# Which engine makes the low parts of PEER's query weights, and which bounds the forget gate

## The chip, the cores and the metric

One core of one Trainium2 chip runs the whole program in one launch. The metric is the device time of that core in microseconds (us); the number reported is the median of the runs. TensorE does matmuls, VectorE and GpSimd elementwise work (GpSimd can't reach PSUM here and is not asked to), ScalarE activations and copies with rounding, SyncE (SP) issues all loads.

## The reference, cut to what matters

Two blocks follow each other on 256 tokens of width 1024, in float32. The first has a mixer (gated linear attention and sparse attention), a cross attention and a PEER layer; the second has a mixer (HGRN2 and Hyena) and another PEER layer. Two places matter here.

A PEER layer computes queries from the normalized activations, scores them against sub-keys, picks 16 experts a head, and sums their outputs:

```
q = (xt @ wq).reshape(N, H, 2, PEER_DKEY // 2)
s = einsum('nhpd,hpkd->nhpk', q, subkeys)      # then top-k twice, softmax
act = gelu(einsum('cd,chkd->chk', xc, down[ec])) * gate
y   = einsum('chk,chkd->cd', act, up[ec])
```

The first PEER layer has 1024 query columns, the second 2048. The second mixer's forget gate is, for forward and backward and for each of 8 heads of 128 channels:

```
logf = log(lb + (1.0 - lb) * sigmoid(z))
k    = (1.0 - lb) * sigmoid(-z)
```

## The kernel before

Activations lie with channels on the partitions: 8 chunks of 128 channels by 256 tokens. Every weight matrix is cut into units of 512 KB (128 partitions by 1024 values). Float32 precision is kept by splitting: a value is the sum of a high part (rounded to fp32r) and a low part (the rest), and a product is three matmuls, L370 (high x high), L371 and L372. A unit of 128 output channels takes 8 chunks x 3 = 24 matmuls of 256 columns.

A unit goes through four hands (`Split`, from L315): SP loads it into one of 3 ring slots (L334), ScalarE copies it rounded to the high part (L338), then an engine subtracts: ring minus high gives the low part. That is VectorE at L343 or GpSimd at L349, as `c.low_by` says when the unit is planned. The ring slot is free when the low part is made. High and low go to one of 3 pairs of buffers, free when TensorE is done with the unit. Two units are fetched ahead of the one that is multiplied (`AHEAD = 2`). A `Whole` unit (L312) is not split; its matmuls (L402) take it from the ring slot in plain float32.

A program is a list of steps in one order. Each engine walks through that list and does its share of each step, with semaphore waits between engines; so the list fixes the order on each engine, and an engine that waits holds up everything behind it.

`late_channels` (L436) runs a projection whose input norm is not known yet: matmuls of the unnormalized activations start at once, and the evacuation `Late` (L552, VectorE) multiplies what is in PSUM by the reciprocal root. The first two units of such a stage are fetched ahead by the stage before it. After the second, `Rstd` (L623, L630, L625) computes the norm. From unit 2 on, evacuations alternate with the steps that `make_norm` gave, spread over the units: here the eight chunks of `NormalizeChunk`, each L711 on VectorE (h times gain times norm), L718 on ScalarE (high part) and L714 on VectorE (low part). L711 and L714 read two operands from SBUF; L552 reads one from PSUM and one from SBUF.

`late_channels` is used in three stages that matter:

- PEER 1 queries (`peer`, 8 units): two chunks a unit, units 2 to 5.
- The keys of the second mixer (16 units): the evacuation is `HgrnKeys`, that is L552, ScalarE's two sigmoids L2327 and L2328, and GpSimd's three instructions L2332 (one_minus times z plus lb), L2333 (one_minus times k) and L2335 (z at least 2^-62). `HgrnLogs` (L2346) takes the logarithm later, of all heads at once. Beside the chunks there are eight `NormInPlace` (L698, VectorE, two SBUF operands), in turns with them.
- PEER 2 queries (`peer`, 16 units): one chunk a unit, units 2 to 9.

Behind the queries `peer` flushes the first two units of the expert table `down`, so they too are split by whatever `c.low_by` says then. Before, that is VectorE; the change to GpSimd comes after the routing is planned, for the rest of the 128 units of `down`. During `down` the routing (top-k) runs on VectorE.

Of the kernel before, what the change touches and what calls it, by code (L numbers as in the profile page):

```python
# [32 lines left out]
ALU = mybir.AluOpType  # L33
ACT = mybir.ActivationFunctionType
# [90 lines left out]
class Step:  # L125
# [10 lines left out]
    def scalar(self, q):  # L136
        pass
# [4 lines left out]
    def pool(self, q):  # L142
        pass
# [292 lines left out]
def late_channels(c, srcs, acts, evac, make_norm, beside=()):  # L436


    beside, waiting = list(beside), []

    def make(unit, n):
        step = c.plan(LateChannels(c, unit, acts, evac(n)))
        waiting.append(step)
        if n == 1:
            beside.extend(make_norm())
        if n >= 1:
            while waiting:
                c.plan(waiting.pop(0))
        if n >= 2:
            for _ in range(-(-len(beside) // max(1, len(srcs) - 2 - n))):  # L450
                c.plan(beside.pop(0))

    for n, src in enumerate(srcs):
        c.submit(src, lambda unit, n=n: make(unit, n))
# [69 lines left out]
class Keep(Evac):  # L524
# [5 lines left out]
    def out_of_psum(self, c):  # L530
        self.kept = c.mark("kept")
        c.last_kept = self.kept
        return self.kept
# [1645 lines left out]
def peer(c, h, xn, work, tmp, gained, squares, name, gain, half_dim, wq, subkeys, down, up, following=()):  # L2179

    n_q = 2 * PEER_H * half_dim // P
    with ExitStack() as ctx:
        x = Experts()
        x.experts = c.sb(name + "_experts", [P, NKEYS, T], ctx)
        x.gates_high = c.sb(name + "_gates_high", [P, T], ctx, F32R)
        free = work[:, :, :].rearrange("p k t -> p (k t)")
        x.pairs, x.gates_low = free[:, 0:2 * T].rearrange("p (a t) -> p a t", a=2), free[:, 2 * T:3 * T]
        x.copy = free[:, 3 * T:3 * T + GROUP * NKEYS].rearrange("p (n t) -> p n t", t=GROUP)
        first_kept = 70
        area = x.experts[:, first_kept:NKEYS, :].rearrange("p a t -> p (a t)")  # L2190
        sk = area[:, 0:n_q * P].rearrange("p (k n) -> p k n", k=n_q)
        qs = area[:, n_q * P:n_q * (P + T)].rearrange("p (k t) -> p k t", k=n_q)
        sk_came = c.load(sk, subkeys, after=[c.last_product])

        def norm():
            c.plan(SumSquares(c, squares, KD - 1))
            c.plan(Rstd(c, tmp[:, :]))
            return [NormalizeChunk(c, h, gain, work, tmp[:, :], xn, k) for k in range(KD)]

        late_channels(c, [wq[n] for n in range(n_q)], gained, lambda n: Late(qs[:, n, :], 1.0, c), norm)  # L2200
        c.flush(down[0], down[1])
        r = Routing(c, area[:, n_q * (P + T):], half_dim, qs, sk, [c.last_kept, sk_came], x.pairs, x.gates_high, x.gates_low)
        x.iota_copied = r.iota_copied = c.plan(CopyIota(c)).copied
        routes = [Route(c, r, i) for i in range(NT)]
        for i in range(4):
            c.bank_free[i] = (routes[1].kept,)
        c.bank_free[6] = (routes[1].kept,)
        places = {3: routes[0:1], 5: routes[1:2], 39: routes, 41: routes}
        x.there, x.gated, x.stored, x.routed = 0, 0, None, r.kept
        c.rotation = [4, 5]  # L2210
        c.low_by = "pool"
        with ExitStack() as inner:
            x.first = c.sb(name + "_first_keys", [P, 2, GROUP, P], inner, F32R)
            x.second = c.sb(name + "_second_keys", [P, 2, GROUP, 2, P], inner, F32R)
            x.hot_free, x.low_made, x.copy_free = [(), ()], None, None
            n_groups, used, finished, first = T // GROUP, 0, 0, 43
            onehots = []
            for n in range(NKEYS):
                for route in places.get(n, ()):
                    c.plan(route)  # L2220
                due = n_groups * (n - first + 1) // (NKEYS - 2 - first)
                new = len(onehots)
                while len(onehots) < min(due, n_groups):
                    onehots.append(c.plan(Onehots(c, x, len(onehots))))
                c.channels(down[n], xn, Hidden(x, n, (r.kept,) if n >= first_kept else ()))
                while used < new:
                    spread = c.plan(Spread(c, x, used, onehots[used]))
                    c.plan(ApplyGates(c, x, used, spread))
                    used += 1
                while finished < len(onehots):  # L2230
                    c.plan(onehots[finished])
                    finished += 1
            c.low_by = "vector"
            c.flush(up[0], up[1])

        x.n_coef = 2
        x.coef = c.sb(name + "_coef", [P, x.n_coef, 2, T], ctx, F32R)
        x.coef_free = [tuple(x.hot_free[0] + x.hot_free[1])] * x.n_coef
        coefs = [None] * NKEYS
        for n in range(NKEYS):  # L2240
            def make(unit, n=n):
                if n == NKEYS - 2:
                    coefs[n + 1] = c.plan(Coef(c, x, n + 1))
                c.plan(UpUnit(c, x, unit, n, coefs[n]))

            if n == 0:
                coefs[0] = c.plan(Coef(c, x, 0))
            elif n >= c.AHEAD:
                coefs[n - c.AHEAD + 1] = c.plan(Coef(c, x, n - c.AHEAD + 1))
            c.submit(up[n], make)  # L2250
        c.flush(*following)
# [56 lines left out]
class HgrnKeys(Evac):  # L2308
# [6 lines left out]
    def out_of_psum(self, c):  # L2315
        self.late = Late(self.z, 1.0, c)
        taken = self.late.out_of_psum(c)
        self.sigmoids, self.scaled = c.mark("hg_sigmoids"), c.mark("hg_scaled")
        self.bounded = c.last_bounded = c.mark("hg_bounded")
        return taken  # L2320

# [3 lines left out]
    def scalar(self, q, out, done):  # L2325
        q.wait_ge(self.late.scaled)
        q.e.activation(self.k, self.z, ACT.Sigmoid, scale=-1.0)  # L2327
        q.e.activation(self.z, self.z, ACT.Sigmoid).then_inc(*self.sigmoids.once())  # L2328

    def pool(self, q, out, done):  # L2330
        q.wait_ge(self.sigmoids, self.bound_ready)
        q.e.tensor_scalar(self.z, self.z, self.one_minus, self.lb, ALU.mult, ALU.add).then_inc(*self.scaled.once())  # L2332
        q.e.tensor_scalar(self.k, self.k, self.one_minus, None, ALU.mult)  # L2333
        q.wait_ge(self.scaled)
        q.e.tensor_scalar(self.z, self.z, 2.0 ** -62, None, ALU.max).then_inc(*self.bounded.once())  # L2335


# [727 lines left out]
def program(nc, dram, out):  # L3065
    with ExitStack() as ctx:
# [27 lines left out]
        with ExitStack() as shared:  # L3094
# [3 lines left out]
            squares = cross_attention(c, h, xn, work, tmp, mem_kv, spare, squares,  # L3098
                                      [dram["peer_wq"][0], dram["peer_wq"][1]])
        peer(c, h, xn, work, tmp, spare, squares, "peer_1", c.gain("norm_ffn"), 64, dram["peer_wq"], dram["peer_subkeys"],  # L3100
             dram["peer_down"], dram["peer_up"], [dram["w_in_2"][8], dram["w_in_2"][9]])

# [13 lines left out]
        def two_norms():  # L3116
            for k in range(KD):
                c.plan(SumGained(c, by_gain, squared[k], k))
            for k in range(KD):
# [6 lines left out]
        c.rotation = list(range(6))  # L3126
        spare, squares = second_mixer(c, h, xn, work, gained, two_norms, [dram["peer_w_q_2"][0], dram["peer_w_q_2"][1]])
        peer(c, h, xn, work, tmp, spare, squares, "peer_2", c.gain("norm_ffn_g_2"), 128, dram["peer_w_q_2"],
             dram["peer_subkeys_2"], dram["peer_u_2"], dram["peer_v_2"])
        with ExitStack() as between:  # L3130
# [115 lines left out]
```

## Time and profile before

| what | value |
|---|---|
| median of 3 runs | 2531.92 us (2531.15 to 2541.61) |
| the profiled execution | 2539.18 us, span 2537.4 us |
| TensorE, VectorE, ScalarE, GpSimd busy | 94%, 65%, 53%, 31% of the span |
| low parts on VectorE (L343) | 398, mean 1228 ns |
| low parts on GpSimd (L349) | 276, mean 2442 ns |
| a 512 KB load, issue to landing | 3.6 us (median, PEER 2 query weights) |
| mean granted TensorE clock | 0.966 |

Busy time is what instructions of an engine cover; a busy TensorE isn't one at its peak. Times in rows are from the start of the span. In a timeline row the first number is the start, the second the duration from the first instruction's start to the last one's end (x2 means two instructions merged), and brackets hold the idle time of the engine before it and what ended it.

### The profile page before, as it was taken

The page shows a single profiled execution, that of the slowest core. Times are in us where ns is not written, and L with a number is a line of the kernel's source. Part 1 is how long each engine was busy: PE and PEld are TensorE (multiplying, and loading weights), DVE is VectorE, ACT ScalarE, POOL GpSimd, SP SyncE. Part 2 cuts the span into 40 slices and gives each one's busy share as a digit, 9 for nine tenths or more (in the row PEclk, how much of TensorE's full clock was granted, in tenths as well). Part 3 has the DMA queues.
Part 4 walks back from the last instruction along what each step waited for, and adds up shares of the span by engine and source line. Part 5 has one row for each costly group of instructions (what it writes and reads, how often), then busy time and mean ns, then how long its engine had stood idle before and what let it go on. Part 6 is the DMA issues. An engine that isn't in the chain of part 4 may idle for free.

```text
span 2537.4 us, 39066 instructions
## 1 busy us (share of the span) xinstructions
PE 2375.6 (94%) x15354; PEld 2140.5 (84%) x15354; DVE 1660.1 (65%) x3193; ACT 1343.1 (53%) x2494; POOL 775.4 (31%) x404
## 2 busy tenths in 40 slices
PE   6878898999999999998888988899999999999998
PEld 5876788999999888886857976799999999788886
DVE  4564456977777556665667384666977778555555
ACT  3345344468887454444433444244468888444443
POOL 3000002877776000000800152101877777000000
PEclk8888899999999999999999998999999999999999
DMA  5322234555555656664332342254555555565563
GB/s 172 124 95 69 92 100 149 176 176 165 165 164 170 185 191 192 192 192 128 125 116 93 116 148 95 67 165 151 183 175 166 162 164 169 180 189 186 189 187 120
DMA packets 108287, 383.36 MB, mean 151 GB/s; under 512 B 12976, under 2 KB 15841, under 8 KB 107529
## 3 DMA queue, kind: packets, MB, share of 16 engines
q1 hardware_dynamic: 108104, 380.86, 47.3%
q8 instruction: 123, 2.02, 0.3%
q14 instruction: 60, 0.48, 0.1%
HBM read 379.74 MB, written 1.06 MB: 150 GB/s over the span
## 4 chain that ended last, share of the span: by engine, by line
PE 81%; DVE 11%; ACT 4%; DMA 2%; issue 2%; POOL 0%; SPq 0%; DVEq 0%; ACTq 0%; POOLq 0%
PE psum L370 23%; PE psum L372 22%; PE psum L371 22%; PE psum L2021 2%; PE psum L402 2%; DVE weight_parts L343 2%; ACT weight_parts L338 2%; PE psum L607 1%; PE psum L2466 1%; PE psum L2686 1%; PE psum L1457 1%; PE psum L1018 1%; PE psum L1357 0%; DVE hg_tmp L1064 0%; PE psum L2611 0%
## 5 line engine op out<-in xcount | busy, mean ns | idle before, releaser
L349 POOL TENSOR_TENSOR weight_parts<-weight_ring,weight_parts 128x1024 fp32r<-128x1024 f32 x276 | 670.8, 2442 | 506.5 <-ACT weight_parts L338 506.0
L370 PE MATMUL psum<-acts_high,weight_parts 128*128 128x256 f32 x2744 | 794.1, 289 | 23.4 <-DVE weight_parts L343 11.2
L338 ACT ACTIVATE weight_parts<-weight_ring 128x1024 fp32r<-128x1024 f32 x674 | 710.6, 1055 | 150.1 <-PE psum L372 79.2
L372 PE MATMUL psum<-acts_high,weight_parts 128*128 128x256 f32 x2744 | 782.6, 285 | 0.0
L371 PE MATMUL psum<-acts_low,weight_parts 128*128 128x256 f32 x2744 | 782.1, 285 | 0.0
L343 DVE TENSOR_TENSOR weight_parts<-weight_ring,weight_parts 128x1024 fp32r<-128x1024 f32 x398 | 488.4, 1228 | 296.1 <-ACT weight_parts L338 295.5
L370 PEld LDWEIGHTS psum<-acts_high,weight_parts 128*128 128x128 f32 x2744 | 532.1, 194 | 34.6 <-issue 12.5
L371 PEld LDWEIGHTS psum<-acts_low,weight_parts 128*128 128x128 f32 x2744 | 532.4, 194 | 1.4 <-issue 0.5
L372 PEld LDWEIGHTS psum<-acts_high,weight_parts 128*128 128x128 f32 x2744 | 532.4, 194 | 0.0
L370 PE MATMUL psum<-weight_parts,peer_coef 128*128 128x512 f32 x1024 | 405.9, 396 | 4.0 <-issue 3.9
L372 PE MATMUL psum<-weight_parts,peer_coef 128*128 128x512 f32 x1024 | 404.8, 395 | 0.0
L371 PE MATMUL psum<-weight_parts,peer_coef 128*128 128x512 f32 x1024 | 402.8, 393 | 0.0
L2103 ACT ACTIVATE peer_coef<-peer_experts 128x256 fp32r<-128x256 f32 x256 | 106.8, 418 | 356.5 <-PE psum L372 355.4
L370 PEld LDWEIGHTS psum<-weight_parts,peer_coef 128*128 128x128 f32 x1024 | 193.4, 189 | 46.5 <-issue 4.2
L372 PEld LDWEIGHTS psum<-weight_parts,peer_coef 128*128 128x128 f32 x1024 | 193.3, 189 | 45.3
L371 PEld LDWEIGHTS psum<-weight_parts,peer_coef 128*128 128x128 f32 x1024 | 193.2, 189 | 44.3
L2107 DVE TENSOR_TENSOR peer_coef<-peer_experts,peer_coef 128x256 fp32r<-128x256 f32 x256 | 108.5, 425 | 153.6 <-ACT peer_coef L2103 153.6
L2002 ACT ACTIVATE peer_second_keys<-psum,work 128x128 fp32r<-128x128 f32 x512 | 146.2, 371 | 14.9 <-DVE peer_second_keys L1993 13.7
L585 POOL TENSOR_TENSOR work<-h 128x256 f32<-128x256 f32 x32 | 19.4, 614 | 410.7 <-DVE h L569 399.5
L2082 ACT ACTIVATE peer_experts<-psum 128x256 f32<-128x256 f32 (+35 forms) x250 | 78.2, 313 | 121.1 <-PE psum L372 121.0
L1990 DVE TENSOR_TENSOR psum<-psum,work 128x512 f32<-128x512 f32 x128 | 89.2, 697 | 59.7 <-ACT peer_second_keys L2002 58.6
L370 PE MATMUL psum<-acts_spare_high,weight_parts 128*128 128x256 f32 x352 | 103.2, 293 | 16.9 <-DVE weight_parts L343 16.8
(426 smaller groups left out, 3135.4 us busy)
## 6 DMA issues: line engine op xcount, KB each, us to landing
weight_ring<-in_peer_down SPq DMA_DIRECT2D x128, 512.0 KB, 3.6
weight_ring<-in_peer_up SPq DMA_DIRECT2D x128, 512.0 KB, 3.5
weight_ring<-in_peer_u SPq DMA_DIRECT2D x128, 512.0 KB, 3.6
weight_ring<-in_peer_v SPq DMA_DIRECT2D x128, 512.0 KB, 3.5
weight_ring<-in_w_in SPq DMA_DIRECT2D x88, 512.0 KB, 3.6
weight_ring<-in_w_out SPq DMA_DIRECT2D x16, 512.0 KB, 3.6
weight_ring<-in_peer_w_q SPq DMA_DIRECT2D x16, 512.0 KB, 3.6
weight_ring<-in_w_in_v SPq DMA_DIRECT2D x10, 512.0 KB, 3.6
```

The lines of the kernel that those rows point to most:

```text
L338: q.e.activation(self.high, self.ring, ACT.Copy).then_inc(*self.rounded.once())
L343: q.e.tensor_tensor(self.low, self.ring, self.high.bitcast(F32), ALU.subtract).then_inc(*self.unit.ready.once())
L349: q.e.tensor_tensor(self.low, self.ring, self.high.bitcast(F32), ALU.subtract).then_inc(*self.unit.ready.once())
L370: q.e.matmul(out, sh, mh, start=first, stop=False)
L371: q.e.matmul(out, sh, ml, start=False, stop=False)
L372: return q.e.matmul(out, sl, mh, start=False, stop=last)
L402: last = q.e.matmul(self.out, w[:, k, :], acts.whole[:, k, :], start=k == 0, stop=k == KD - 1)
L1990: q.e.tensor_tensor(ones, iota, over(x.pairs[:, 1, tokens], P, 2), ALU.is_equal).then_inc(*self.marked.once())
L2002: last = q.e.activation(self.second[:, t, 1, :], self.c.bank(6)[:, P * t:P * t + P], ACT.Copy, bias=0.0, scale=x.gates_low[:, token:token ...
L2082: last = q.e.activation(self.x.experts[:, self.n, n:T], out[:, n:T], ACT.Gelu_apprx_tanh)
L2103: q.e.activation(self.high, self.src, ACT.Copy).then_inc(*self.rounded.once())
L2107: q.e.tensor_tensor(self.low, self.src, self.high.bitcast(F32), ALU.subtract).then_inc(*self.ready.once())
```

## The change

The line `c.low_by = "pool"` in `peer` moves up, ahead of the query projection, so that query units 2 and up and the first two units of `down` are split by GpSimd. In `HgrnKeys` the instruction z = one_minus * z + lb moves from GpSimd (L2332) to ScalarE, as an Identity activation with scale and bias from memory, behind a wait for ScalarE's own sigmoid. GpSimd's multiplication of k stays and no longer has the other ahead of it; its maximum waits for the Identity.

```diff
@@ peer
+        c.low_by = "pool"
         late_channels(c, [wq[n] for n in range(n_q)], gained, lambda n: Late(qs[:, n, :], 1.0, c), norm)
         c.flush(down[0], down[1])
...
         c.rotation = [4, 5]
-        c.low_by = "pool"
@@ HgrnKeys
-        self.sigmoids, self.scaled = c.mark("hg_sigmoids"), c.mark("hg_scaled")
+        self.sigmoids, self.forgets = c.mark("hg_sigmoids"), c.mark("hg_forgets")
...
         q.e.activation(self.z, self.z, ACT.Sigmoid).then_inc(*self.sigmoids.once())
+        q.wait_ge(self.sigmoids, self.bound_ready)
+        q.e.activation(self.z, self.z, ACT.Identity, bias=self.lb, scale=self.one_minus).then_inc(*self.forgets.once())
 
     def pool(self, q, out, done):
         q.wait_ge(self.sigmoids, self.bound_ready)
-        q.e.tensor_scalar(self.z, self.z, self.one_minus, self.lb, ALU.mult, ALU.add).then_inc(*self.scaled.once())
         q.e.tensor_scalar(self.k, self.k, self.one_minus, None, ALU.mult)
-        q.wait_ge(self.scaled)
+        q.wait_ge(self.forgets)
         q.e.tensor_scalar(self.z, self.z, 2.0 ** -62, None, ALU.max).then_inc(*self.bounded.once())
```

## Rows read from the trace of the kernel before

**Rows 1.** Busy by window: length, then PE, PEld, DVE, ACT, POOL; clock, DMA.

```profile
398.97:417.73 18.76, 12.00 (x96) 11.21 (x97) 12.79 (x25) 8.45 (x14) 0.00 (x0) 1.00 0.33 113
...
1717.08:1740.79 23.71, 21.40 (x169) 19.99 (x169) 16.65 (x29) 10.53 (x15) 0.00 (x0) 1.00 0.49 156
1740.79:1751.80 11.01, 11.01 (x97) 11.01 (x98) 7.67 (x10) 4.25 (x4) 0.00 (x0) 1.00 0.77 226
...
1223.56:1254.60 31.04, 27.23 (x217) 25.62 (x218) 19.41 (x33) 16.38 (x33) 29.57 (x28) 1.00 0.48 153
1254.60:1282.20 27.60, 27.60 (x130) 24.31 (x129) 18.12 (x25) 8.30 (x12) 7.97 (x9) 1.00 0.44 134
```

**Rows 2.** Timeline of VectorE, one unit of PEER 2's queries.

```profile
1719.19 1.23 DVE L343 TENSOR_TENSOR weight_parts<-weight_ring,weight_parts 128x1024 fp32r<-128x1024 f32 x1 [0.53 <-ACT weight_parts L338]
1720.33 0.42 DVE L552 SCALAR_TENSOR_TENSOR peer_experts<-psum,tmp 128x256 f32<-128x256 f32 x1
1720.67 0.47 DVE L711 SCALAR_TENSOR_TENSOR work<-h,gains,tmp 128x256 f32<-128x256 f32 x1
1721.62 0.43 DVE L714 TENSOR_TENSOR acts_low<-work,acts_high 128x256 fp32r<-128x256 f32 x1 [0.48 <-ACT acts_high L718]
1722.58 1.23 DVE L343 TENSOR_TENSOR weight_parts<-weight_ring,weight_parts 128x1024 fp32r<-128x1024 f32 x1 [0.52 <-ACT weight_parts L338]
```

**Rows 3.** Timeline of ScalarE in the same unit.

```profile
1721.17 0.42 ACT L718 ACTIVATE acts_high<-work 128x256 fp32r<-128x256 f32 x1 [2.02 <-DVE work L711]
1721.50 1.04 ACT L338 ACTIVATE weight_parts<-weight_ring 128x1024 fp32r<-128x1024 f32 x1
```

**Rows 4.** Waits of TensorE, 1207.5 to 1254.6: us in total, times, longest.

```profile
PE psum L370 <- DVE weight_parts L343: 4.2, 9, 0.7
```

**Rows 5.** Timeline of VectorE, keys: the first and last of eleven low parts.

```profile
1214.77 1.37 DVE L343 TENSOR_TENSOR weight_parts<-weight_ring,weight_parts 128x1024 fp32r<-128x1024 f32 x1
...
1250.47 1.23 DVE L343 TENSOR_TENSOR weight_parts<-weight_ring,weight_parts 128x1024 fp32r<-128x1024 f32 x1 [0.53 <-ACT weight_parts L338]
```

**Rows 6.** Timeline of GpSimd: low parts beside VectorE's work.

```profile
418.39 3.01 POOL L349 TENSOR_TENSOR weight_parts<-weight_ring,weight_parts 128x1024 fp32r<-128x1024 f32 x1 [32.74 <-ACT weight_parts L338]
...
1499.35 4.72 POOL L349 TENSOR_TENSOR weight_parts<-weight_ring,weight_parts 128x1024 fp32r<-128x1024 f32 x2 [5.46 <-ACT weight_parts L338]
```

**Rows 7.** Timeline of ScalarE, then TensorE: unit 2 of PEER 2's queries.

```profile
1705.56 1.06 ACT L338 ACTIVATE weight_parts<-weight_ring 128x1024 fp32r<-128x1024 f32 x1 [5.19 <-DMA weight_ring<-in_peer_w_q]
...
1707.92 0.39 PE L370 MATMUL psum<-acts_spare_high,weight_parts 128*128 128x256 f32 x1 [2.04 <-DVE weight_parts L343]
```

**Rows 8.** Timeline of VectorE beside the low parts of Rows 6.

```profile
417.93 1.22 DVE L343 TENSOR_TENSOR weight_parts<-weight_ring,weight_parts 128x1024 fp32r<-128x1024 f32 x1
...
1500.28 0.48 DVE L2806 SCALAR_TENSOR_TENSOR hy_u<-psum,gains,hy_u 128x255 f32<-128x255 f32 x1
...
1502.46 1.89 DVE L1065 SCALAR_TENSOR_TENSOR work<-work,gains,hg_tmp 128x256 f32<-128x256 f32 x1
```

**Rows 9.** Timeline of ScalarE, keys: the second sigmoid and what follows.

```profile
1231.49 0.40 ACT L2328 ACTIVATE hg_zf<-hg_zf 128x256 f32<-128x256 f32 x1
1231.80 1.04 ACT L338 ACTIVATE weight_parts<-weight_ring 128x1024 fp32r<-128x1024 f32 x1
```

**Rows 10.** Timeline of VectorE: L678 waits for VectorE's own L677.

```profile
1201.94 0.41 DVE L677 TENSOR_SCALAR both<-psum 128x256 f32<-128x256 f32 x1
1202.39 0.42 DVE L678 SCALAR_TENSOR_TENSOR both<-tmp,both 128x256 f32<-128x256 f32 x1
```

**Rows 11.** Timeline of ScalarE: an Identity with scale and bias from memory, its follower.

```profile
1477.68 0.55 ACT L2796 ACTIVATE hy_x<-psum,gains 128x256 f32<-128x256 f32 x1
1478.13 0.71 ACT L1040 ACTIVATE hg_sq<-work 128x256 f32<-128x256 f32 x2
```

**Rows 12.** Timeline of GpSimd, then VectorE, in the keys.

```profile
1213.34 0.85 POOL L2335 TENSOR_SCALAR hg_zf<-hg_zf 128x256 f32<-128x256 f32 x1
...
1213.82 0.43 DVE L714 TENSOR_TENSOR acts_low<-work,acts_high 128x256 fp32r<-128x256 f32 x1 [0.71 <-ACT acts_high L718]
```

## Prediction

> **What bounds the kernel now.** I read the page's busy shares first (TensorE 94% of the span), which says little about three stretches of some 30 us, so I went to the stretches that the diff touches, with busy time by window [rows 1]. "Unit" is one weight block of 512 KB: a load, a high part on ScalarE (L338), a low part (L343 on VectorE, L349 on GpSimd), 24 matmuls. Where nothing holds TensorE up, four units take 11.01 us, 2.75 each, TensorE busy throughout at a granted clock of 1.00 (as in all five windows). PEER-1's query stage (398.97 to 417.73, 4 units) needs 4.69 a unit and TensorE works 12.00 of 18.76; PEER-2's (1717.08 to 1740.79, 7 units) 3.39 a unit. Both wait for a low part on VectorE. The period is a ring of VectorE and ScalarE, each of which takes its instructions in order, to be seen in the timeline [rows 2, 3]: L343 starts 1719.19, L552 1720.33, L711 1720.67, ScalarE's L718 1721.17, its next L338 1721.50, the next L343 1722.58: 3.39. PEER-1 has two norm chunks (L711, L718, L714) a unit, hence 4.69.
>
> The third stretch is the forget-gate keys. TensorE waits for L343 nine times, once a unit [rows 4]. Its ring is L343, L552, ScalarE's two sigmoids L2327 and L2328, perhaps L718, then L338 and L343 again: ten periods in 1250.47 - 1214.77 = 35.70 us [rows 5]. GpSimd is nearly full here (29.57 of 31.04) but nobody on the ring waits for it. Behind it TensorE is busy for all 27.60 us [rows 1], so what the keys lose is lost to the end.
>
> **Part 1, low parts on GpSimd.** Prefetched units 0 and 1 of each query stage stay on VectorE; 6 + 14 query units and 2 + 2 units of the first expert table move: 24 L343 at 1.23 us go, 24 L349 at about 2.4 come (4.72 for two [rows 6]). No load is added. SP's queue gets its slot free about 1.2 us later per unit; three slots against a load of 3.6 (median of the page's list of loads), L338 of 1.05 and 2.4 make 7.1 / 3 = 2.4 us a unit, under 2.75, so the queue is covered.
>
> If GpSimd and VectorE ran side by side the ring would lose 1.2 us. Unit 2 would start 1.2 later (L338 begins 1705.56, TensorE 1707.92 [rows 7]; +1.17 for 2.4 instead of 1.23), then run at 2.75 to 2.8: PEER-2's first expert unit at 1709.1 + 14 x 2.8 = 1748.3 against 1751.8, 3.5 gained. In PEER-1 the ring of evacuation and two chunks takes 2.92 (L552 0.34, twice L711 to L714 0.95 and L714 0.34); following units 5, 6, 7 and the first expert unit through gives 412.2 against 417.73, 5.5 gained.
>
> But the rows say they don't run side by side. GpSimd's two L349 from 1499.35 end at 1504.07; VectorE's L1065, two operands in SBUF, issued at 1502.46, takes 1.89, where the like L711 takes 0.47 [rows 2], and ends 0.28 after that, while L2806 at 1500.28, whose other operand is in PSUM, takes its 0.48 [rows 6, 8]. The other way round, L349 at 418.39 behind L343 (417.93, 1.22) takes 3.01 and ends 2.25 after it. So L711 and L714 (both operands in SBUF) wait for a running L349, L552 (PSUM) doesn't. The Trainium skill, SBUF — State Buffer, "Who interferes with whom", says the same: a VectorE instruction with two SBUF inputs contends with a GpSimd instruction that reads SBUF, and the later one blocks fully; by this rule the 9.0 us above are not to be had.
>
> Worked through from these durations. PEER-2: let L711 be issued at L. By [rows 2, 3] L711 comes L718 + 0.45 (L714) + 0.34 + 0.34 = 1.13 after L718, GpSimd's low part 0.33 + 1.08 = 1.41 after it, so L711 is first by 0.28 and the low part runs L+0.48 to L+2.73. L714, issued L+0.96, ends L+3.01. Having waited, it goes ahead of the next low part, which runs to L+5.26. The next L711, issued L+3.27, ends L+5.54; L718 L+5.57; L714 L+6.02, free; L552 L+6.36; L711 L+6.70. Two units in 6.7: 3.35 each, against 3.39. From the first chunk (L = 1715.45 once unit 4's low part has held chunk 0 back) unit 12 starts 1740.85 + 0.2 for handshakes, against 1740.79, then 11.0 us to the experts: +0.3. PEER-1: with two chunks a unit the same steps give L711 at L+2.95 for the second chunk, L718 L+3.46, L714 L+3.91, L552 L+4.25, the next L711 L+4.59: 4.59 against 4.69; unit 5 starts 0.2 late, the first expert unit 0.3 early. Part 1 together: 0. Bounds: -9.0 with no blocking; +9.4 if L711 loses the race each time. Then a period is 0.3 + 0.37 + 1.08 + 2.4 = 4.15 in PEER-2 (8 x 0.77 = 6.1) and 5.5 in PEER-1 (4 x 0.82 = 3.3). I take 0, the race being won by 0.28. No L711 or L714 of before runs beside an L349, so the order of issue is worked out, not seen.
>
> **Part 2, the bound on ScalarE.** L2332 leaves GpSimd 16 times, which nobody misses. ScalarE gets one Identity a unit, which first waits for its own sigmoid. Before, what follows L2328 starts 0.31 after it [rows 9]. Now: the sigmoid's full 0.40, 0.04 for an engine's wait on itself (L677 takes 0.41 and L678 starts 0.45 after it [rows 10]), then the Identity. With scale and bias from memory it has a pitch of 0.45 (L2796 at 1477.68, next at 1478.13 [rows 11]). 0.40 + 0.04 + 0.45 - 0.31 = 0.58 a unit. Queued behind it are L718 and L338, for which VectorE and TensorE wait. L338 of units 5 to 15 follows the Identities of 2 to 12: 11 x 0.58 = 6.4. Those of units 0 and 1 are hidden, since VectorE then waits for TensorE to end unit 2, whatever ScalarE does. L343 lasts 1.37 at 1214.77 and 1.23 at 1250.47 [rows 5]; less GpSimd work beside it may return 0.05 a unit in some eight of them, 0.4. Bounds: 11 x 0.31 = 3.4 if the wait is free, 11 x 0.64 = 7.0 if it costs 0.1. I take +6.0. The later logarithms and scans lie beside the 27.60 us of matmuls.
>
> A block would be possible here too. Counted from L552, the new ring has the sigmoid's end at 1.18, L2333 on GpSimd from 1.2 to 2.15, the Identity's end at 1.77, L2335 from 2.25 to 3.10, L714 at 2.12, L698 issued at 2.46 and L343 due at 3.06. If L2335 held VectorE over its whole recorded span, L698 would end at 3.4 and L343 start 0.3 late in the eight units with a chunk, +2.4. But L714 at 1213.82 takes its usual 0.43 although L2335 is recorded from 1213.34 to 1214.19 [rows 12]: a 256-element GpSimd instruction doesn't hold VectorE over its recorded span. I take 0 for it. The same section of the Trainium skill has the lock last for the whole instruction, which this row doesn't bear out.
>
> **Sum.** 0 + 6.0 = +6.0 on the profiled execution: span 2537.4 to 2543.4, its time 2539.2 to 2545.2. It was 7.3 above the median of the runs, by more than the change; I carry the difference to the median: 2531.9 + 6.0 = 2538. About 0.5% (12.7 us) is what can be told from no change.
>
> **Rivals.**
> No blocking in the query stages (the low parts then run beside the chunks): -9.0 + 6.0 = -3, 2529. For it: L714 beside L2335. Against: L1065's 1.89. Chance 0.15.
> L711 loses the race: L711 starts only when a low part ends, and every period is a serial chain of both engines. +9.4 + 6.0 = +15.4, 2547, slower. It decides when L711 is issued after L349, that is from 0.28 us of delay on VectorE. For it: the margin is small and rests on pitches. Against: after a block L714 and L552 bring L711 into step again. Chance 0.10.
> The Identity is hidden, because GpSimd's relief shortens the ring: 0, 2532. For it: GpSimd is 95% busy. Against: the ring holds no GpSimd instruction. Chance 0.12.
> L2335 holds L698 in the keys for its whole span: 6.0 + 2.4 = +8.4, 2540. Against it: L714 beside L2335. The Trainium skill's section named above would have it so. Chance 0.08.
>
> **How the numbers follow.** Forecast 0.55: 2538, within 0.5%. Range: down to the first rival, 2528, up to the second, 2548; the shown runs lie 10 us apart, which is in it too. Faster by over 0.5%: only with luck of the runs, 0.03. Slower by over 0.5%: the second rival, and a little of the forecast with high runs, 0.11. Same 0.86.
>
> **What would show it.** The first low part of the first expert table is in L349. L711 and L714 have maxima near 2.4 us in the query stages, alternating with normal ones, and the period of PEER-2 stays at 3.3 to 3.4, with TensorE waiting for L349. In the keys the period of L343 grows by 0.58, the last key unit starts some 6 us later counted from 1207.57, and GpSimd no longer lags. Wrong would be: periods of 2.8 in the queries; 4 or more there; or the keys' ten periods still at 35.7.

## The result, and the profile after

The changed kernel takes 2541.01 us (median of 20 runs, 2536.46 to 2548.06) against 2533.27 us for the kernel before on the same chip (20 runs, 2529.99 to 2541.61). The ratio is 1.0028 with a 95% interval of 1.0020 to 1.0035, so the change costs 7.1 us (5.1 to 8.9). The predicted 2538 was +6.0 on the base of that time, 2531.9. One of run 12's twelve executions took 3015.4 us at a granted clock of 0.72, against about 0.96 in all others, and is left out of its ratio.

The two profiled spans differ by less, 2538.7 against 2537.4 us, and that must be cleared up before any row is compared. From PEER-2's first expert unit to the end of the span, where TensorE is as busy in both and the change touches only one low part that nobody waits for, before took 785.6 us and after 777.2. Of the fourteen executions profiled in this study (a kernel run twice counts twice), two took 785.6 and twelve 777.2 to 778.9, for kernels that are the same there. The profiled execution of before was one with a slow last stretch, which fits its 7.3 us above the median. So I read the change stage by stage. A query stage is counted from TensorE's first matmul with `acts_spare` to its first with `acts_high`, which is the first expert unit; the keys from the stage's first L343 to TensorE's first L402.

| stage, us | before | after | difference | predicted |
|---|---|---|---|---|
| PEER-1's queries | 33.15 | 32.62 | -0.5 | -0.3 |
| PEER-2's queries | 52.35 | 54.17 | +1.8 | +0.3 |
| the keys | 64.97 | 71.11 | +6.1 | +6.0 |
| sum | | | +7.4 | +6.0 |

The sum lies within the interval of the measured 7.1.

**PEER-2's queries.** First the timeline of the three engines (start, length, engine, line, tiles; in brackets the idle time before and who ended it), from the evacuations of units 2 and 3 to a full pair of units. Line numbers below 2200 are those of before.

```profile
1721.45 0.42 DVE L552 SCALAR_TENSOR_TENSOR peer_experts<-psum,tmp 128x256 f32<-128x256 f32 x1 [1.55 <-PE psum L372]
1721.79 0.47 DVE L711 SCALAR_TENSOR_TENSOR work<-h,gains,tmp 128x256 f32<-128x256 f32 x1
...
1723.75 2.40 POOL L349 TENSOR_TENSOR weight_parts<-weight_ring,weight_parts 128x1024 fp32r<-128x1024 f32 x1 [2.33 <-ACT weight_parts L338]
1724.18 0.42 DVE L552 SCALAR_TENSOR_TENSOR peer_experts<-psum,tmp 128x256 f32<-128x256 f32 x1 [1.00 <-PE psum L372]
1724.52 1.91 DVE L711 SCALAR_TENSOR_TENSOR work<-h,gains,tmp 128x256 f32<-128x256 f32 x1
...
1727.59 0.47 DVE L711 SCALAR_TENSOR_TENSOR work<-h,gains,tmp 128x256 f32<-128x256 f32 x1
1727.91 4.93 POOL L349 TENSOR_TENSOR weight_parts<-weight_ring,weight_parts 128x1024 fp32r<-128x1024 f32 x2 [1.76 <-ACT weight_parts L338]
...
1728.55 2.04 DVE L714 TENSOR_TENSOR acts_low<-work,acts_high 128x256 fp32r<-128x256 f32 x1 [0.48 <-ACT acts_high L718]
1730.36 0.38 PE L370 MATMUL psum<-acts_spare_high,weight_parts 128*128 128x256 f32 x1 [0.78 <-POOL weight_parts L349]
1730.51 0.41 DVE L552 SCALAR_TENSOR_TENSOR peer_experts<-psum,tmp 128x256 f32<-128x256 f32 x1
1730.85 2.28 DVE L711 SCALAR_TENSOR_TENSOR work<-h,gains,tmp 128x256 f32<-128x256 f32 x1
...
1733.61 0.43 DVE L714 TENSOR_TENSOR acts_low<-work,acts_high 128x256 fp32r<-128x256 f32 x1 [0.48 <-ACT acts_high L718]
```

Against [rows 2] the low part has left VectorE, and what it left behind is waiting. From 1727.59 on, L711 takes 0.47, 2.28, 0.47 and so on, and L714 takes 2.04 after a short L711 and 0.43 after a long one. A long one ends 0.28 us or so after the low part that it met (1723.75 + 2.40 = 1726.15; 1724.52 + 1.91 = 1726.43). This is the alternation that was worked out ahead, with 6.7 us for a pair of units: every second unit of TensorE starts at 1730.36, 1737.07, 1743.76 and 1750.44, which makes pairs of 6.71, 6.69 and 6.68.

What is new stands before it. Three windows of TensorE (columns as in [rows 1]) around unit 2's start:

```profile
1712.00:1717.00 5.00, 1.91 (x14) 1.51 (x14) 0.42 (x1) 3.48 (x4) 2.60 (x2) 1.00 0.64 260
1717.00:1721.00 4.00, 4.00 (x23) 4.00 (x23) 2.51 (x3) 1.28 (x2) 4.00 (x2) 0.58 0.60 169
1721.00:1725.00 4.00, 4.00 (x37) 4.00 (x36) 2.06 (x5) 1.37 (x2) 1.67 (x2) 0.99 0.60 228
```

and the wait ahead of them:

```profile
1716.80 0.39 PE L370 MATMUL psum<-acts_spare_high,weight_parts 128*128 128x256 f32 x1 [3.09 <-POOL weight_parts L349]
```

TensorE waits 3.09 us for unit 2's low part, where it waited 2.04 before [rows 7]. Then the granted clock falls to the lower of its two levels, 1.2 GHz, for most of 4 us (0.50 over 1717.64 to 1721.05): 23 matmuls in 4 us instead of 37, and 14 x 4 / 37 = 1.5 us lost. Before, the same unit ran at the upper level:

```profile
1708.00:1712.00 4.00, 4.00 (x35) 4.00 (x36) 3.48 (x4) 2.59 (x3) 0.00 (x0) 1.00 0.64 197
```

The late matmuls also made L552 wait for TensorE, for unit 2 until 1721.45 and for unit 3 until 1724.18. So the second L711 was issued after the low part of 1723.75, lost the race for the order of issue once, and took 1.91.

**PEER-1's queries** run at 4.53 us a unit (TensorE starts units at 403.09, 407.62, 412.15 and 416.68), every second L714 at 2.02 to 2.04, and no L711 is held. TensorE's waits from 398 to 417 us:

```profile
PE psum L370 <- POOL weight_parts L349: 5.1, 4, 1.5
```

The granted clock fell once in this stage too, behind unit 2, although TensorE had waited only 1.89 us for it (a window from its start on):

```profile
392.38:396.38 4.00, 4.00 (x22) 4.00 (x23) 2.47 (x3) 2.40 (x3) 3.80 (x2) 0.61 0.57 156
```

In the second profile of the same kernel (run 10) the wait was 2.00 us and the clock stayed at 1.00. That stage is 0.4 us shorter there.

**The keys.** The timeline of one unit without a chunk, ScalarE, GpSimd and VectorE:

```profile
1242.09 0.42 ACT L2327 ACTIVATE hg_kb<-hg_zb 128x256 f32<-128x256 f32 x1 [1.63 <-DVE hg_zb L552]
1242.41 0.40 ACT L2328 ACTIVATE hg_zb<-hg_zb 128x256 f32<-128x256 f32 x1
1242.85 0.60 ACT L2330 ACTIVATE hg_zb<-hg_zb,hg_lb,hg_one_minus 128x256 f32<-128x256 f32 x1
1242.90 0.94 POOL L2334 TENSOR_SCALAR hg_kb<-hg_kb,hg_one_minus 128x256 f32<-128x256 f32 x1 [2.23 <-ACT hg_zb L2328]
1243.35 1.05 ACT L338 ACTIVATE weight_parts<-weight_ring 128x1024 fp32r<-128x1024 f32 x1
1243.91 0.85 POOL L2336 TENSOR_SCALAR hg_zb<-hg_zb 128x256 f32<-128x256 f32 x1
1244.43 1.23 DVE L343 TENSOR_TENSOR weight_parts<-weight_ring,weight_parts 128x1024 fp32r<-128x1024 f32 x1 [1.99 <-ACT weight_parts L338]
```

The Identity (L2330) starts 0.44 after its sigmoid, and L338 follows it 0.50 later; in [rows 9] L338 followed the sigmoid by 0.31. The units with a chunk now come every 4.25 us and those without every 3.94 (before 3.68 and 3.30), so ten periods take 1256.86 - 1215.33 = 41.53 us against the 35.70 of [rows 5]. GpSimd, which was nearly full, waits for ScalarE over 2 us a unit and nobody gains by it. TensorE's waits in the stage (us in total, times, longest), where [rows 4] had 4.2 in 9:

```profile
PE psum L370 <- DVE weight_parts L343: 10.4, 10, 1.2
```

### The profile page after: what moved, and what is told of

It reads as the page before. It is cut to its first block, busy times and chain, and to the rows that moved or that the text cites. A ratio compares the mean times of both kernels' runs of the same rounds, so it can differ in the third digit from the quotient of the medians.

```text
span 2538.7 us, 39067 instructions
## 1 busy us (share of the span) xinstructions
PE 2370.9 (93%) x15354; PEld 2141.9 (84%) x15354; DVE 1648.0 (65%) x3169; ACT 1352.5 (53%) x2510; POOL 812.3 (32%) x412
## 3 DMA queue, kind: packets, MB, share of 16 engines
q8 instruction: 123, 2.02, 0.3%
## 4 chain that ended last, share of the span: by engine, by line
PE 81%; DVE 11%; ACT 4%; issue 2%; DMA 2%; POOL 1%; SPq 0%; DVEq 0%; ACTq 0%; POOLq 0%
PE psum L370 23%; PE psum L372 22%; PE psum L371 22%; PE psum L2021 2%; PE psum L402 2%; DVE weight_parts L343 1%; PE psum L607 1%; ACT weight_parts L338 1%; PE psum L2687 1%; PE psum L2467 1%; POOL weight_parts L349 1%; PE psum L1457 1%; PE psum L1018 1%; DVE acts_low L714 1%; PE psum L1357 0%
## 5 line engine op out<-in xcount | busy, mean ns | idle before, releaser
L349 POOL TENSOR_TENSOR weight_parts<-weight_ring,weight_parts 128x1024 fp32r<-128x1024 f32 x300 | 727.2, 2436 | 456.1 <-ACT weight_parts L338 455.8
L338 ACT ACTIVATE weight_parts<-weight_ring 128x1024 fp32r<-128x1024 f32 x674 | 710.5, 1055 | 147.1 <-PE psum L372 73.9
L343 DVE TENSOR_TENSOR weight_parts<-weight_ring,weight_parts 128x1024 fp32r<-128x1024 f32 x374 | 458.4, 1227 | 277.4 <-ACT weight_parts L338 277.3
```

The costliest lines, as they stand in the source:

```text
L338: q.e.activation(self.high, self.ring, ACT.Copy).then_inc(*self.rounded.once())
L343: q.e.tensor_tensor(self.low, self.ring, self.high.bitcast(F32), ALU.subtract).then_inc(*self.unit.ready.once())
L349: q.e.tensor_tensor(self.low, self.ring, self.high.bitcast(F32), ALU.subtract).then_inc(*self.unit.ready.once())
```

## The experiments

All were timed in five rounds beside the kernel before. "Stages" are the three differences to before in the order of the table above. The unedited rest moved between executions: the start by up to 9 us, and the stretch from the keys to PEER-2 by some 4. So a time tells some 3 to 4 us apart, a stage some 0.7.

**1. Part 1 alone.** Only the move of `c.low_by = "pool"`.

```diff
+        c.low_by = "pool"
         late_channels(c, [wq[n] for n in range(n_q)], gained, ...
...
-        c.low_by = "pool"
```

> Part 1 alone: the low parts of both query stages on GpSimd, the keys as before. Theory (GpSimd's low part and VectorE's L711/L714 exclude each other, the order settles into a fixed alternation; the traces of before and after differ by -0.53 us in PEER-1's queries and +1.83 in PEER-2's): +1.3 us against before, pairs of units 6.7 us apart in PEER-2. Rival, no blocking: -9. Rival, L711 loses every time: +9.4.

Measured: ratio 1.0001 (0.9987 to 1.0016), +0.3 us (-3.3 to +4.1); stages -1.0, +1.8, -0.3. PEER-2's L711 takes up to 2.28 and L714 up to 2.06. Both rivals lie outside the interval: the stages together neither gain 9 us nor lose them.

**2. Part 2 alone.** Only the edits in the keys.

> Part 2 alone: the Identity on ScalarE, the query stages' low parts on VectorE. Theory (11 periods of the keys' ring grow by the sigmoid's full length, the engine's wait on itself and the Identity's pitch, 0.57 to 0.64 each): +6.2 us. Rival, the stretch is hidden by TensorE: 0. Rival, the wait on itself is free: 11 x 0.31 = +3.4.

Measured: 1.0031 (1.0016 to 1.0046), +7.9 us (+4.1 to +11.7); stages -0.1, -0.1, +6.5, ten periods 41.53 us. Hidden, and a free wait, are outside the interval. Nearly the whole loss is this part's.

**3 and 4. The lock taken away.** In run 3 the chunks' product and a copy of the rms factor lie in PSUM and the low parts stay on VectorE; in run 4 the low parts move as well.

```diff
+class ChunkInPsum(NormalizeChunk):
...
+        self.x, self.gain, self.out, self.tmp = x[:, k, :], gain[:, k:k + 1], c.bank(7)[:, 0:T], c.bank(7)[:, T:2 * T]
...
+class RstdCopied(Rstd):
...
+        q.e.reciprocal(self.tmp, self.tmp).then_inc(*self.ready.once())
+        q.wait_ge(self.ready)
+        settle(self.c, q, "vector", q.e.tensor_copy(self.c.bank(7)[:, T:2 * T], self.tmp))
...
-            return [NormalizeChunk(c, h, gain, work, tmp[:, :], xn, k) for k in range(KD)]
+            return [ChunkInPsum(c, h, gain, xn, k) for k in range(KD)]
```

> The kernel before with the norm chunks' product and its rms factor in a PSUM bank, so that L711 and L714 each have one operand in SBUF; low parts stay on VectorE. This is the control of the next run. Theory: no GpSimd instruction contends in the query stages before, so nothing changes but the lengths: one copy of about 0.4 us twice, and up to 0.1 us a chunk if the PSUM operand is slower: 0 to +1.5 us.

Measured: 1.0013 (0.9998 to 1.0029); stages -0.3, +0.3, +0.1. This was the other execution with 785.6 us in the last stretch. By its stages the move into PSUM by itself is worth nothing.

> Part 1 alone, with the product and the rms factor of the norm chunks in PSUM. If the exclusion of L349 against two-SBUF-operand instructions is what took the gain: L711 and L714 stay near 0.5 us at their longest, PEER-2's units come every 2.75 to 2.8 us (first expert unit 3.5 us earlier), PEER-1's every 2.9 to 3.2 (5.5 us earlier), together about -9 + 1 = -8 us. Rival, VectorE is held whatever its operands' place: +1.3 to +3, pairs of 6.7 us stay. Rival, the period was bound by something else (ScalarE's order, the slots): periods above 3.2 in PEER-2 with short L711 and L714.

Measured: 0.9974 (0.9958 to 0.9989), -6.6 us (-10.7 to -2.8); stages -5.0, -2.9, +0.2. The timeline of PEER-2's queries:

```profile
1716.23 2.41 POOL L349 TENSOR_TENSOR weight_parts<-weight_ring,weight_parts 128x1024 fp32r<-128x1024 f32 x1 [0.32 <-ACT weight_parts L338]
1716.68 0.42 DVE L552 SCALAR_TENSOR_TENSOR peer_experts<-psum,tmp 128x256 f32<-128x256 f32 x1 [1.02 <-PE psum L372]
1717.02 0.48 DVE L711 SCALAR_TENSOR_TENSOR psum<-h,gains,psum 128x256 f32<-128x256 f32 x1
...
1717.95 0.42 DVE L714 TENSOR_TENSOR acts_low<-psum,acts_high 128x256 fp32r<-128x256 f32 x1 [0.45 <-ACT acts_high L718]
1718.95 2.40 POOL L349 TENSOR_TENSOR weight_parts<-weight_ring,weight_parts 128x1024 fp32r<-128x1024 f32 x1 [0.31 <-ACT weight_parts L338]
```

L711 is issued 0.79 us into a running low part and takes 0.48; both are as short as alone. The period is 2.72, L552 waits for TensorE in every unit, and TensorE is the bound. Against the pair above each has one operand fewer in SBUF. L711's output left SBUF as well, but in run 9 below it is back there and L711 still takes 0.47, so it is the inputs that count. With that the exclusion is shown, and where part 1's gain went. The Trainium skill, SBUF — State Buffer, "Who interferes with whom", says that a VectorE instruction with at most one SBUF input, outside the modes that use two ports, does not contend with GpSimd; these rows agree. PEER-1 gained 5.0 of the expected 5.5 us and PEER-2 2.9 of 3.5. TensorE's wait for unit 2 was 3.25 us here and the clock fell as in the changed kernel (0.73 over 1702 to 1708).

**5 and 6. The price on ScalarE.** In run 5 ScalarE takes k's multiplication, whose sigmoid came first; in run 6 both steps.

```diff
-        q.wait_ge(self.sigmoids, self.bound_ready)
-        q.e.activation(self.z, self.z, ACT.Identity, bias=self.lb, scale=self.one_minus).then_inc(...)
+        q.wait_ge(self.first, self.bound_ready)
+        q.e.activation(self.k, self.k, ACT.Copy, bias=0.0, scale=self.one_minus).then_inc(...)
```

> The changed kernel, but the multiplication that ScalarE takes over is that of k by one_minus, whose sigmoid came first, and z's two-pointer step stays on GpSimd. If 0.13 of the 0.64 us a unit is ScalarE waiting for the sigmoid just before, that part goes: ten periods of L343 take 41.53 - 1.3 = 40.2 us, +4.7 in the keys against before, about +6 in all. Rival, the wait is no part of the price: 41.5 us stay. Rival, a shorter list of pointer operands makes the instruction cheaper too: under 39.5.

> The changed kernel with both steps on ScalarE: k by one_minus, then z's Identity, which by then need not wait; GpSimd keeps the maximum alone. Theory (the keys' ring grows by the pitches on ScalarE, whatever GpSimd is relieved of): 0.51 + 0.51 a unit, ten periods 35.70 + 9.6 = 45.3 us, some +10.3 in the keys and +11.5 in all, so about 1.0045. Rival, GpSimd's relief gives something back on the ring (L343 shorter, no contention): under 44.

Measured: run 5 0.9997 (0.9982 to 1.0011), stages -0.9, +2.4, +3.6, ten periods 1252.06 - 1212.89 = 39.17 us; run 6 1.0023 (1.0009 to 1.0037), stages -0.7, +2.0, +9.0, ten periods 44.08. Timeline of ScalarE in run 6, one unit:

```profile
1238.52 0.40 ACT L2329 ACTIVATE hg_zb<-hg_zb 128x256 f32<-128x256 f32 x1
1238.83 0.49 ACT L2331 ACTIVATE hg_kb<-hg_kb,hg_one_minus 128x256 f32<-128x256 f32 x1
1239.23 0.59 ACT L2333 ACTIVATE hg_zb<-hg_zb,hg_lb,hg_one_minus 128x256 f32<-128x256 f32 x1
1239.72 0.40 ACT L718 ACTIVATE acts_high<-work 128x256 fp32r<-128x256 f32 x1
```

Both misses have one cause: the step with one pointer operand has a pitch of 0.40 (1238.83 to 1239.23), not the 0.51 that I had given it, and the Identity with two pointers 0.49. Neither waits for the sigmoid, since 0.31 after the last sigmoid's start there was other work to do. So the Identity's 0.64 is 0.13 of waiting and 0.51 of pitch; run 5's 0.40 a unit is what the rival with the shorter list of pointers had said (the step is also a Copy and no Identity, which these runs don't separate). In run 6 the ring grows by 0.40 + 0.49 = 0.89 (3.30 to 4.19) and GpSimd's further relief gives nothing back beyond the first 0.07.

**7. The race, made to be lost.** Part 1 alone, with two short VectorE instructions ahead of each L711.

```diff
+        q.e.tensor_scalar(self.spare[:, 0:T], self.tmp, 1.0, None, ALU.mult)
+        q.e.tensor_scalar(self.spare[:, T:2 * T], self.tmp, 1.0, None, ALU.mult)
         super().vector(q)
```

> Part 1 alone, with two short VectorE instructions (rms factor into an unused PSUM bank, one SBUF operand each) ahead of every L711, which issue it at least 0.4 us later. If the race decides: L711 loses each time, PEER-2's units with a chunk come every 4.15 us instead of 3.35 and PEER-1's every 5.5 instead of 4.53, together 7 to 9 us slower than part 1 alone, +8 to +11 against before. Rival, the alternation is stable against such a delay: periods grow by the added instructions at most, to 3.75 in PEER-2, +3 in all.

Measured: 1.0038 (1.0020 to 1.0056), +9.6 us (+5.1 to +14.2); stages +5.6, +7.5, -0.1. Two units of PEER-2, GpSimd and VectorE:

```profile
1736.70 2.37 POOL L349 TENSOR_TENSOR weight_parts<-weight_ring,weight_parts 128x1024 fp32r<-128x1024 f32 x1 [1.76 <-ACT weight_parts L338]
1737.04 2.31 DVE L711 SCALAR_TENSOR_TENSOR work<-h,gains,tmp 128x256 f32<-128x256 f32 x1
...
1740.82 2.37 POOL L349 TENSOR_TENSOR weight_parts<-weight_ring,weight_parts 128x1024 fp32r<-128x1024 f32 x1 [1.76 <-ACT weight_parts L338]
1741.16 2.32 DVE L711 SCALAR_TENSOR_TENSOR work<-h,gains,tmp 128x256 f32<-128x256 f32 x1
```

L711 is issued 0.34 us after the low part and loses in every unit; the period is 4.12 to 4.13. The serial chain of the second rival is real. The two instructions add nothing to it but the later issue: L711 ends 0.28 us after the low part. In PEER-1 units come every 6.18 us, above the expected 5.5, because the second chunk's two instructions stand in the ring too. With that the stages come to +13.0, above the expected 8 to 11.

**8 and 11. Unit 2's low part left on VectorE**, on top of run 4 (`low_from` is 3).

```diff
     for n, src in enumerate(srcs):
+        if n == low_from:
+            c.low_by = "pool"
         c.submit(src, lambda unit, n=n: make(unit, n))
```

> Part 1 with the chunks' product and rms factor in PSUM, and unit 2 of each query stage left on VectorE, which is idle then. Expected from 2.4 against 1.23 us for the first low part that TensorE waits for: the stage of PEER-1 26.9 us instead of 28.1, PEER-2's 48.3 instead of 49.5, so 2.4 us more than the run without this, about -9 to -10 against before (0.9963). Rival, the units behind it then wait for GpSimd and give it back: no better than -6.6.

> The kernel with the chunks' product and rms factor in PSUM and unit 2 on VectorE once more. By its stages -3.8 (of which 1.9 were lost to a lower granted clock in one unit) and -3.9: -8 to -10 us against before, not the -14.5 first measured.

Measured: 0.9943 (0.9925 to 0.9961) and 0.9963 (0.9950 to 0.9976), -14.5 and -9.4 us; stages -3.8, -3.9, -0.3 and -3.7, -4.6, -0.3. PEER-2 gains another 1.0 us over run 4 in run 8 and 1.7 in run 11, and its clock holds, as the wait and two windows of run 8 show:

```profile
1704.11 0.38 PE L370 MATMUL psum<-acts_spare_high,weight_parts 128*128 128x256 f32 x1 [2.06 <-DVE weight_parts L343]
```

```profile
1702.00:1706.00 4.00, 1.95 (x17) 1.89 (x17) 1.72 (x3) 3.75 (x5) 1.84 (x1) 1.00 0.53 183
1706.00:1710.00 4.00, 4.00 (x37) 4.00 (x37) 3.51 (x6) 1.16 (x3) 2.97 (x2) 1.00 0.75 240
```

PEER-1 lost 1.2 us to run 4 instead of gaining 1.2, and 1.3 in run 11. In both, TensorE had to wait 2.49 us for unit 5, against 2.23 in run 4, so part of what unit 2 had gained was given back, as the rival says. The clock then fell, which it had not done in run 4:

```profile
400.00:403.00 3.00, 1.85 (x12) 1.85 (x13) 2.06 (x6) 1.72 (x3) 2.35 (x2) 0.83 0.25 42
403.00:406.00 3.00, 3.00 (x18) 3.00 (x18) 0.93 (x3) 1.33 (x2) 2.38 (x2) 0.60 0.64 172
```

This is the fastest version of the study: some 10 us under the kernel before, and 0.5% under the changed one (0.9963 against 1.0014, timed side by side).

**9. Only the rms factor in PSUM**, the rest as in run 8: L711 has one SBUF operand, L714 again two.

> As the run with unit 2 on VectorE, but only the rms factor lies in PSUM: L711 has one SBUF operand, L714 again two. If it is L711's place ahead of ScalarE's high parts that matters, and L714 may wait as long as L552 has to wait for TensorE anyway: in PEER-2 L714 takes up to 1.1 us and the units still come every 2.7 to 2.8 us, the stage 48.5 to 49.5; in PEER-1 the second chunk's L711 stands behind a held L714, so the period is 4.0 to 4.5 and the stage 31 to 32. Together -4 to -5 us against before. Rival, any held instruction brings the 3.35 back: PEER-2 at 52 or more, about -1 in all.

Measured: 0.9966 (0.9953 to 0.9979), -8.6 us (-11.9 to -5.3); stages -0.3, -4.1, 0.0. Timeline of PEER-2 (L713 and L716 are L711 and L714 two lines further down):

```profile
1732.64 0.47 DVE L713 SCALAR_TENSOR_TENSOR work<-h,gains,psum 128x256 f32<-128x256 f32 x1
...
1733.60 0.97 DVE L716 TENSOR_TENSOR acts_low<-work,acts_high 128x256 fp32r<-128x256 f32 x1 [0.48 <-ACT acts_high L720]
1734.60 2.41 POOL L349 TENSOR_TENSOR weight_parts<-weight_ring,weight_parts 128x1024 fp32r<-128x1024 f32 x1 [0.30 <-ACT weight_parts L338]
1735.02 0.42 DVE L554 SCALAR_TENSOR_TENSOR peer_experts<-psum,tmp 128x256 f32<-128x256 f32 x1 [0.45 <-PE psum L372]
```

The low half of the chunk is held for half a microsecond and costs nothing, because the evacuation behind it has to wait for TensorE anyway. The period is 2.72 as in run 4. In PEER-1, where the second chunk stands behind the held instruction, the period stays at 4.52 and the stage takes 32.9 us; 4.0 to 4.5 and 31 to 32 were expected. So in PEER-2 it is enough to free L711, the one that ScalarE's high parts hang on. The time is 4 us below what the stages say (-4.4), and its interval excludes them.

**10 and 12. Two kernels again**, the changed one and that of run 5.

> The changed kernel once more, on the same chip as the other three, since the times of the runs before came out up to 5 us below the sum of their stages: +7.1 as first measured (1.0028), its stages -0.5, +1.8 and +6.1 us.

> The changed kernel with k's multiplication on ScalarE in place of z's Identity, once more. By its stages (-0.9, +2.4, +3.6) +5 us against before and 2.1 less than the changed kernel. First measured: -0.8, with an interval from -4.6 to +2.8. If the stages tell all, it comes out between +3 and +6; if not, something behind the keys gives time back.

Measured: the changed kernel 1.0014 (1.0005 to 1.0024), +3.6 us (+1.3 to +6.1), stages -0.9, +2.5, +6.2; that of run 5 1.0027 (1.0010 to 1.0044), +6.8 us (+2.5 to +11.2), stages -0.7, +1.9, +3.5, where +3 to +6 was expected. The stages repeat to 0.7 us, the times less well: the changed kernel came out at +7.1 and now at +3.6, that of run 5 at -0.8 and now at +6.8. Between two kernels closer than that, the stages decide. In runs 5, 6, 8, 9 and 10 the sum of the stages lies outside the interval of the time, by 0.9 to 2.2 us, and each time the time is the lower one. The kernel before was slower then, too (medians of 2536.2 and 2535.9 against 2533.3); whether more of its executions had the slow last stretch can't be told, since one profile of it was kept. What moves the unedited rest is open.

## Why the prediction was right, and where its sizes were off

**The bound and the place of each part.** Right. Query stages and keys were bound by rings of VectorE and ScalarE, and all of the change's difference lies in these three stages.

**Part 1, no gain because L349 and the chunks exclude each other.** Right, and shown: with the exclusion the stages gave +0.7 us in run 1, without it -7.9 in run 4. The 9.0 us that the prediction bounded this by were nearly all there to be had, but not by this change. The alternation came as worked out: 6.7 us a pair in PEER-2, and 4.53 instead of 4.59 a unit in PEER-1. That a little delay turns the order of issue is shown by run 7, where L711 came 0.34 us after the low part and 4.13 us a unit came for the predicted 4.15.

**PEER-2, "+0.3".** Mis-sized: +1.8 in the changed kernel, +1.8 to +2.5 in the other executions with the exclusion and no added instructions. The step "unit 2 would start 1.2 later" was right (2.04 to 3.09 us of waiting), and its consequence was not followed up. I took the matmuls behind the longer wait at the clock of before. Over the fourteen executions the rows are of one mind: in the eight where unit 2's low part was GpSimd's, TensorE waited 3.1 to 3.5 us for it and the granted clock was then 0.57 to 0.64 over the next 4 us; in the six where it was VectorE's, TensorE waited 1.9 to 2.1 us and the clock stayed at 1.00. Run 8 and run 4 differ in this edit alone. Behind unit 2, TensorE lost the 1.5 us worked out above. A second step was off as well: I let unit 4's low part hold chunk 0 back and the alternation start from there. In fact chunk 0 went free (L711 at 1721.79 took 0.47), and the first meeting was that behind unit 3's L552, lost for the late matmuls. But that, too, follows from the clock: L711 could only go once unit 2's L552, which waited 1.55 us for TensorE, had gone at 1721.45. At the upper clock unit 2's 24 matmuls take 2.75 us, so L711 would have been issued near 1720.2, into unit 4's low part (1719.04 to 1721.41), as predicted. The alternation would then have started as predicted, and unit 12, which started 1.6 us later than forecast (1750.44 against 1741.05, with the stage itself starting 7.82 later), would have been in time. This is an estimate from the rows: no run has the exclusion with unit 2's low part on VectorE.

**Part 2, "11 x 0.58 - 0.4 = +6.0".** Right in sum, in part by luck, since two errors cancel. The Identity's pitch beside its follower is 0.50 to 0.51 and not 0.45, so a unit costs 0.64; the sigmoid's full length and the wait on it (0.44) were right. Where a chunk stands, L343 gives back the 0.05 to 0.07 that were taken for the contention that goes, and the period grows by 0.57. But eleven periods were counted and ten grew so, by 5.83 in all; the one ahead of them went from 4.99 to 5.14 us only. With 0.08 at either end of the stage that is the 6.1.

**L2335 holding L698 (now L2336).** L698 does take 0.62 instead of 0.47 beside it in four of its eight places, a touch and not the recorded span of 1.0, and L343 still starts on its due time, 0.03 behind L338. Taking 0 was right, and the ten periods leave no room for the +2.4.

**The other rivals.** No blocking and the hidden Identity are refuted by runs 1 and 2. The lost race happened once in PEER-2 and then not again. **The base.** I carried the difference to the median; since the profiled execution of before was slow in a stretch behind the change, that was the right way.

## What to carry to other kernels

Before work moves from VectorE to GpSimd, list the VectorE instructions with two operands in SBUF that will lie beside it. Beside low parts of 2.4 us they waited for the end of the GpSimd instruction when they came second, and what they held up took the whole gain back. Putting one operand in PSUM frees them; first free the one that another engine waits for (run 9). Keeping the first item, for which the others idle, on the fast engine paid in PEER-2 and not in PEER-1 (runs 8 and 11), so look at what waits behind it. An instruction appended to a ring costs its pitch, and if it needs the result of the one ahead also the overlap that this one had (0.51 and 0.13 us here), whoever is relieved elsewhere.

## What the runs showed of the hardware

- In PEER-2's query stage one microsecond more of waiting (2.0 to 3.1 us) was followed by 3.4 us at 1.2 GHz, in eight executions of eight. To TensorE that is 1.1 us of waiting and 1.5 of slower matmuls; of this, runs 8 and 11 got 1.0 and 1.7 back in the stage. The length of the wait alone doesn't decide: in PEER-1 waits of 2.49 us (runs 8 and 11), 2.22 (run 9) and 1.89 (the changed kernel) were followed by the lower clock, and waits of 2.23 (run 4), 2.17 (run 6) and 2.00 (run 10) were not.
- A held VectorE instruction goes ahead of the next low part, and makes it late by little: two low parts in a row with a held L714 between them take 4.93 us, against the 4.72 of [rows 6], and that L714 ends at 1730.59, 0.29 us after the first of the two.
- ScalarE's 128x256 instruction has a pitch of 0.31 with constants, 0.40 with one pointer operand and 0.49 to 0.51 with two, and starts 0.44 after an instruction of its own that it waits for.
- The stretch of expert units up to the end takes 777 to 779 us in twelve executions and 785.6 in two (before and run 3), at a TensorE that is full in both. The difference builds up evenly over the last 380 us or so, in the 512-column matmuls: 859 of them in 200 us against 875, at a granted clock of 1.00 in both. What slows them is open.
